# A hybrid attention layer on one core: queries and keys loaded, and chunked outputs stored, 128 partitions at a time

## The reference, cut to what matters

```
proj = x @ w_in                               # aq ak av ag | bq bk bv bg
ya = chunked attention(aq, ak, av, rel_bias)  # 8 heads of 64, own chunk of 64 + 8 before it
ya = ya * silu(ag)
yb = sliding attention(rope(bq), rope(bk), bv, sinks)   # 8 heads, 2 key/value heads, own chunk + 1 before it
yb = yb * silu(bg)
h  = alpha * x + concat(ya, yb) @ w_out
h  = h + sigmoid(h @ w_gate) * (p @ w_ple)
x  = layer_norm(h)
```

## Time and profile before

| | us |
|---|---|
| median of three runs | 2729.72 (2725.06 to 2730.3) |
| the profiled execution | 2724.94 |
| its span, from the first to the last instruction | 2723.1 |
| TensorE busy in the span | 2592.7 (95%) |
| VectorE busy | 1216.6 (45%) |
| ScalarE busy | 1003.4 (37%) |
| GpSimd busy | 354.4 (13%) |
| mean granted TensorE clock | 0.976 |

### The profile page before, as it was taken

The page is one execution under the profiler, slowest core; times in us unless marked ns, Lnnn a source line. Parts: engine busy times, 40 slices in busy tenths (PEclk is TensorE's granted clock), DMA queues, the critical chain, the costliest instruction groups (busy, mean ns, idle before and its releaser), DMA issues. The chain is left out here.

```text
span 2723.1 us, 38119 instructions
## 1 busy us (share of the span) xinstructions
PE 2592.7 (95%) x14100; PEld 2265.4 (83%) x14100; DVE 1216.6 (45%) x2433; ACT 1003.4 (37%) x2091; POOL 354.4 (13%) x192
## 2 busy tenths in 40 slices
PE   7999999999999999998989998887899999999997
PEld 5888888998888888998989897885688888888886
DVE  5211136341212164167878785775334334334333
ACT  4111112241111122167878786774322222222222
POOL 2000000000000000000000000001343443443441
PEclk9999999999999999999999998888999999999998
DMA  6431246363322265388778769987444444445440
GB/s 199 153 123 65 81 97 137 140 229 116 123 89 73 81 116 147 127 217 199 175 167 195 167 149 216 215 224 198 117 123 112 119 118 117 118 114 122 117 112 31
DMA packets 366843, 377.08 MB, mean 138 GB/s; under 512 B 82920, under 2 KB 291960, under 8 KB 363000
## 3 DMA queue, kind: packets, MB, share of 16 engines
q1 hardware_dynamic: 365816, 374.61, 51.9%
q0 software_dynamic: 896, 0.80, 0.1%
HBM read 240.33 MB, written 136.07 MB: 138 GB/s over the span
## 5 line engine op out<-in xcount | busy, mean ns | idle before, releaser
L1347 PE MATMUL psum<-x_hi,w_hi 128*128 128x512 f32 x1344 | 524.1, 390 | 18.1 <-DVE x_lo L1051 17.7
L1347 PE MATMUL psum<-x_lo,w_hi 128*128 128x512 f32 x1344 | 523.8, 390 | 0.0
L1347 PE MATMUL psum<-x_hi,w_lo 128*128 128x512 f32 x1344 | 523.8, 390 | 0.0
L1347 PEld LDWEIGHTS psum<-x_hi,w_hi 128*128 128x128 f32 x1344 | 252.9, 188 | 70.9 <-issue 17.7
L1347 PEld LDWEIGHTS psum<-x_hi,w_lo 128*128 128x128 f32 x1344 | 252.8, 188 | 52.7
L1347 PEld LDWEIGHTS psum<-x_lo,w_hi 128*128 128x128 f32 x1344 | 252.8, 188 | 52.5
L724 POOL TENSOR_TENSOR y_raw<-y_two 128x512 f32<-128x512 f32 x32 | 41.2, 1286 | 1802.8 <-DMA y_two<-ya_d 1802.8
L1148 DVE CUSTOM_DVE_ANT_0 prob<-psum,bias 128x640 f32<-128x640 f32 (+4 forms) x256 | 199.3, 778 | 91.0 <-issue 90.7
L856 ACT ACTIVATE prob<-prob,small 128x640 f32<-128x640 f32 (+4 forms) x256 | 203.9, 797 | 69.4 <-DVE small L1148 65.2
L1245 DVE TENSOR_TENSOR y_lo<-y_raw,y_hi 128x1024 fp32r<-128x1024 f32 x32 | 39.2, 1226 | 397.1 <-ACT y_hi L885 397.1
L1347 PE MATMUL psum<-wo_hi,y_hi 128*128 128x512 f32 x512 | 202.7, 396 | 1.4 <-DVE wo_lo L1240 1.3
(11 more groups left out here) (163 smaller groups left out, 4878.4 us busy)
## 6 DMA issues: line engine op xcount, KB each, us to landing
qk_d<-stage_out SPq DMA_DIRECT2D x72, 512.0 KB, 2.7
w_raw<-in_w_in SPq DMA_DIRECT2D x20, 1024.0 KB, 5.7
v_d<-stage_out SPq DMA_DIRECT2D x64, 320.0 KB, 2.2
x_raw<-in_xT SPq DMA_DIRECT2D x32, 512.0 KB, 4.8
g_d<-stage_out SPq DMA_DIRECT2D x64, 256.0 KB, 2.0
bq_d<-stage_out SPq DMA_DIRECT2D x64, 256.0 KB, 4.0
ya_d<-y_a SPq DMA_DIRECT2D x128, 128.0 KB, 3.6
bq<-bq_d SPq DMA_DIRECT2D x64, 256.0 KB, 5.4
```

The lines of the kernel that those rows point to most:

```text
L1347: return pe.matmul(dst, lhs, rhs, start=start, stop=stop)
```

## The change

Five transfers or pairs of transfers are redrawn. The semaphores count fewer landings accordingly.

- `load_job`: `aq_hi` and `aq_lo` are each loaded by one transfer that reads every row of the source twice, into neighbouring partitions (a copy dimension of 2 behind the 64 rows). `ak` is loaded by one transfer that puts the high and the low part of a row into neighbouring partitions. Partition order is thus (row, copy) in place of (copy, row), alike for both operands. Four transfers per head or part in place of seven. `aq_lo` is now issued at q = 7 together with the bias.
- `load_bq` and `load_bk`: the same for the sliding stage, one transfer in place of two each.
- The store of `y_a`: all 128 partitions in one transfer, to a scratch tensor `ya_d[head, 128, tokens]`.
- `load_tile`: `y_two` is fetched in four transfers of 64 partitions each, in place of one of 128. Its free dimension is ordered (half, pair) in place of (pair, half), and GpSimd's addition reads it so.

```diff
-        ya_d = scratch("ya_d", [A_HEADS // 2, 2, 2, HEAD, SEQ])
+        ya_d = scratch("ya_d", [A_HEADS, 2 * HEAD, SEQ])
...
             def load_job(head, s, piece, done, t0=0, t1=NT):
 
                 cols = slice(t0 * P, t1 * P)
-                if piece < 4:
-                    dst, c, r0 = ((aq_hi, 0, 0), (aq_hi, 0, HEAD), (aq_lo, 1, 0), (aq_lo, 1, HEAD))[piece]
-                    sp.dma_start(dst[r0:r0 + HEAD, s, cols].bitcast(f32), qk_d[c, bass.ds(head * HEAD, HEAD), cols]
+                n = (t1 - t0) * P
+                if piece < 2:
+                    dst = (aq_hi, aq_lo)[piece]
+                    sp.dma_start(dst[:, s, cols].bitcast(f32),
+                                 qk_d[piece, bass.ds(head * HEAD, HEAD), cols].unsqueeze(1).to_broadcast([HEAD, 2, n])
                                  ).then_inc(done, 16)
-                elif piece < 6:
-                    c = piece - 4
-                    sp.dma_start(ak[c * HEAD:c * HEAD + HEAD, s, cols].bitcast(f32),
-                                 qk_d[c, bass.ds(D_A + head * HEAD, HEAD), cols]).then_inc(done, 16)
+                elif piece == 2:
+                    sp.dma_start(ak[:, s, cols].bitcast(f32),
+                                 qk_d[:, bass.ds(D_A + head * HEAD, HEAD), cols].rearrange("c d t -> d c t")
+                                 ).then_inc(done, 16)
...
-                for piece in range(7):
+                for piece in range(4):
...
-                for c in range(2):
-                    sp.dma_start(bq[c * HEAD:c * HEAD + HEAD, which, block * 2 * TB:(block + 1) * 2 * TB].bitcast(f32),
-                                 bq_d[pair + which, :, s * JB + block, c, :, :, :].rearrange("d n h q -> d (n h q)")
-                                 ).then_inc(bq_loaded[block], 16)
+                sp.dma_start(bq[:, which, block * 2 * TB:(block + 1) * 2 * TB].bitcast(f32),
+                             bq_d[pair + which, :, s * JB + block, :, :, :, :].rearrange("d c n h q -> d c (n h q)")
+                             ).then_inc(bq_loaded[block], 16)
...
-                    for r0 in (0, HEAD):
-                        sp.dma_start(dst[r0:r0 + HEAD, s, cols].bitcast(f32), src).then_inc(bk_loaded[s], 16)
+                    sp.dma_start(dst[:, s, cols].bitcast(f32),
+                                 src.unsqueeze(1).to_broadcast([HEAD, 2, cols.stop - cols.start])).then_inc(bk_loaded[s], 16)
...
                         sp.wait_ge(y_copied, quad0 + q + 1)
-                        for c in range(2):
-                            sp.dma_start(ya_d[bass.ds(it, 1), c, s, :, q * TB:q * TB + TB]
-                                         .rearrange("a d t -> (a d) t"),
-                                         y_a[c * HEAD:c * HEAD + HEAD, q % QSLOTS, :]).then_inc(y_stored[q % QSLOTS], 16)
+                        sp.dma_start(ya_d[bass.ds(head, 1), :, q * TB:q * TB + TB].rearrange("a d t -> (a d) t"),
+                                     y_a[:, q % QSLOTS, :]).then_inc(y_stored[q % QSLOTS], 16)
...
-                sp.dma_start(y_two[:, s, :, :], ya_d[:, :, :, :, cols].rearrange("k c h d t -> (h d) (k c) t")
-                             ).then_inc(y_two_loaded[s], 16)
+                for hd in range(2):
+                    for c in range(2):
+                        sp.dma_start(y_two[hd * HEAD:hd * HEAD + HEAD, s, c * KT // 2:(c + 1) * KT // 2, :],
+                                     ya_d[:, c * HEAD:c * HEAD + HEAD, cols].rearrange("(k h) d t -> h d k t", h=2)[hd]
+                                     ).then_inc(y_two_loaded[s], 16)
```

More of the change, by code:

```diff
@@ L283, in wait_head @@
                 if t % PART == 0:
-                    eng.wait_ge(first_loaded[t // PART], 16 * (9 if t == 0 else 7))
+                    eng.wait_ge(first_loaded[t // PART], 16 * (6 if t == 0 else 4))
             elif t == 0:
-                eng.wait_ge(job_loaded[s], 144 * (turn + s))
+                eng.wait_ge(job_loaded[s], 96 * (turn + s))
         def v_out(slot):
@@ L299, in _ @@
             for sm in y_stored:
-                sp.sem_inc(sm, 32)
+                sp.sem_inc(sm, 16)
             def load_panel(col, width):
@@ L500, in stage_a @@
                         sp.wait_ge(y_copied, quad0 + q + 1)
-                        for c in range(2):
-                            sp.dma_start(ya_d[bass.ds(it, 1), c, s, :, q * TB:q * TB + TB]
-                                         .rearrange("a d t -> (a d) t"),
-                                         y_a[c * HEAD:c * HEAD + HEAD, q % QSLOTS, :]).then_inc(y_stored[q % QSLOTS], 16)
+                        sp.dma_start(ya_d[bass.ds(head, 1), :, q * TB:q * TB + TB].rearrange("a d t -> (a d) t"),
+                                     y_a[:, q % QSLOTS, :]).then_inc(y_stored[q % QSLOTS], 16)
                         if q == 0 and more:
-                            load_job(head + 1, 1 - s, 4, job_loaded[1 - s])
-                            load_job(head + 1, 1 - s, 5, job_loaded[1 - s])
+                            load_job(head + 1, 1 - s, 2, job_loaded[1 - s])
                         if q == 1 and more:
-                            load_job(head + 1, 1 - s, 6, job_loaded[1 - s])
+                            load_job(head + 1, 1 - s, 3, job_loaded[1 - s])
                         if q == QUADS - 2 and load_next:
@@ L515, in stage_a @@
                             load_job(head + 2, s, 0, job_loaded[s])
+                        if q == QUADS - 1 and load_next:
                             load_job(head + 2, s, 1, job_loaded[s])
-                        if q == QUADS - 1 and load_next:
-                            load_job(head + 2, s, 2, job_loaded[s])
-                            load_job(head + 2, s, 3, job_loaded[s])
                             load_bias(head + 2, s, job_loaded[s])
@@ L540, in _ @@
                 first_head(part)
-            for piece in range(4):
+            for piece in range(2):
                 load_job(1, 1, piece, job_loaded[1])
@@ L547, in _ @@
             for stored in y_stored:
-                sp.wait_ge(stored, 32 * (A_HEADS * QUADS // QSLOTS + 1))
+                sp.wait_ge(stored, 16 * (A_HEADS * QUADS // QSLOTS + 1))
             sp.wait_ge(recipT_copied, 1)
@@ L718, in y_tile @@
             def y_tile(t, s, first=False):
-                two = y_two[:, s, :, :].rearrange("p (k c) t -> p k c t", c=2)
-                pool.wait_ge(y_two_loaded[s], 8 * (t - s) + 16)
+                two = y_two[:, s, :, :].rearrange("p (c k) t -> p c k t", c=2)
+                pool.wait_ge(y_two_loaded[s], 32 * (t - s) + 64)
                 if not first:
                     pool.wait_ge(y_split, t - 1)
-                pool.tensor_tensor(y_raw[:, s, 0:KT // 2, :], two[:, :, 0, :], two[:, :, 1, :], ALU.add).then_inc(y_joined, 1)
+                pool.tensor_tensor(y_raw[:, s, 0:KT // 2, :], two[:, 0, :, :], two[:, 1, :, :], ALU.add).then_inc(y_joined, 1)
                 pool.wait_ge(g_loaded[s], 8 * (t - s) + 16)
@@ L845, in a_step @@
                     act.wait_ge(values_done, A_QUADS * it + quad + 1)
-                    act.wait_ge(y_stored[slot], 32 * (A_QUADS // QSLOTS * it + quad // QSLOTS + 1))
+                    act.wait_ge(y_stored[slot], 16 * (A_QUADS // QSLOTS * it + quad // QSLOTS + 1))
                     act.activation(y_a[:, slot, :], psum[:, 6 + quad % 2, :], ACT.Copy).then_inc(y_copied, 1)
@@ L1472, in b_scores @@
                 if u % 4 == 0:
-                    pe.wait_ge(bq_loaded[i // 2], 64 * (u // (2 * B_UNITS) + 1))
+                    pe.wait_ge(bq_loaded[i // 2], 32 * (u // (2 * B_UNITS) + 1))
                 if i == 0:
-                    pe.wait_ge(bk_loaded[s], 64 * (pair // 2 + 1))
+                    pe.wait_ge(bk_loaded[s], 32 * (pair // 2 + 1))
                 if u >= 2:
```

## The result

| | before | after |
|---|---|---|
| median, us | 2727.39 (2724.75 to 2730.3, 4 runs) | 2701.3 (2696.57 to 2701.87, 4 runs) |
| the profiled execution, us | 2724.94 | 2701.23 |
| its span, us | 2723.1 | 2699.4 |
| TensorE busy, us | 2592.7 | 2586.1 (96%) |
| mean granted clock | 0.976 | 0.979 |

The ratio is 0.990, 95% interval 0.9883 to 0.9918: some 26 us by the medians, 23.7 by the two profiled executions. The forecast was 2700, in a range of 2690 to 2719.

What follows compares the result with a forecast made beforehand. Slow 64-partition transfers were held to make TensorE wait in the chunked and sliding stages. Terms -11.1 -1.5 -20 +2.5 = -30 us: 2695 from the profiled 2724.94, 2700 from the median 2729.72; range 2690 to 2719.

Steps and rivals of the forecast that it cites:

- The mechanism: Query and key loads, y_a stores: a busy engine moves 1.6 to 1.9 times as much when transfers span 128 partitions.
- First head and first change: Chunked stage, first head and change to the second: the wait for av and both y_a waits go; gain 11.1 us.
- Start of the sliding stage: TensorE's 4.2 us wait for bq shrinks as its load is issued sooner and moves quicker; gain 1.5 us.
- Body of the sliding stage: VectorE's waits for y_b stores mostly go, and the slower clock with them; gain 20 us, bounds 10 and 22.5.
- at 1745 about 1 us stays: Sliding body: the 4.1 us wait for a y_b store behind bq and v_b shrinks to about 1 us.
- the wait at 1791: Sliding body: a 2.5 us wait for a y_b store was to go (4 us less bq).
- under 3 us: Sign to look for: VectorE's y_b waits before 1840 us total under 3 us.
- y_two in four: End of sliding stage and changeover: three more issues per tile lose 1.25 us at each, together 2.5; steady tiles cost 0.
- 1 (issues only): All changed transfers: width buys no rate, only issues are saved; about 2721 us, chance 0.10.
- 3 (the twice-read source): Loads of aq_hi and aq_lo: copying one HBM place to many partitions is slow; near 2900 us, chance 0.05.
- 2 (the small-run loads are the true cause): SyncE's queue: v_b's and av's 4096 pieces fill it and stay; body gains only 4 to 6; 2715 us, chance 0.11.
- 4 (the last stage): Last stage: the y_two fetch comes onto its path, 31 tiles by 1 us; about 2730 us, chance 0.04.

Runs made afterwards that it cites:

- the kernel with the old count: Against the kernel before: query and key loads 128 partitions wide but cut in two by columns, as many transfers as before, outputs as before; 2701.75 us.
- the kernel with v_b in two: Against the changed kernel: each group's middle v_b load in two parts by columns, the second three steps later; 2697.1 us.

## Why the prediction was right

- *The mechanism.* Forecast: width pays in rate, by the y_a and stage_out rows. Shown, by the kernel with the old count (2701.75) and by that with every second partition (415 GB/s). The wording "two engines sharing a way into one half" is more than was shown; shown is that loads into one half move 218 GB/s at a full share, and loads over both 415 to 422.
- *First head and first change, -11.1.* Measured -11.05, and av's wait is gone; av landed at 1211.98, forecast was 1213. Fewer issues were not needed for it: with the old count the four passes take 28.00 as well.
- *Start of the sliding stage, -1.5.* Measured -2.6; bq's wait went from 4.2 to 2.5, where 2.7 was named. With the loads alone wide it was 3.2, so the single store of y_a has its share in it, as forecast.
- *Body of the sliding stage, -20 within 10 to 22.5.* Measured -14.2. This is the mis-sized term. The step that failed is the last: "at 1745 about 1 us stays", and that the wait at 1791 goes. Both v_b waits stayed, at 1.88 and 2.34 us; their 4.2 us also miss the sign "under 3 us". I had subtracted bq's saving from the old wait. But v_b's issue waits for TensorE's progress, so it doesn't move ahead. What to add up was the queue ahead of the store: 1 MB of bq (3 us at 341 GB/s) and 2 MB of v_b in 512-byte runs (7 us at the 299 of the earlier trace rows). That is 10 us, before the store's own 2 to 3, where the slot is wanted again after two passes, 9.4. With the rate of the strips in the earlier trace rows for bq, this was to be had from the rows. The clock was not the error: 1 us of wait was priced at 2.5 us lost, and 4.2 us of wait left 8.4. Mis-sized was what waits. As the body with slow loads took 121.65 to 125.63 us and with wide ones 106.34 to 108.96, the gain is some 13 to 19 us and the -14.2 of one pair of executions is near its lower end.
- *y_two in four, +2.5.* Two places were to lose 1.25 each. Measured +2.3 at the end of the sliding stage, where the kernels with four transfers lie 2.4 above those with one, and nothing that shows at the changeover: its gap went from 11.98 to 12.15 and the first tile grew by 0.7, but with one transfer and wide loads they are as long or longer (13.38, and 27.05 for the tile's 26.54). The sum is right by luck, as one place was twice as dear and the other free. The gap was named at 12.5 to 14 and stayed under it. In the steady tiles y_two took 3.0 to 3.4 us to issue where it took 0.39, more than the 1.2 to 2.0 added in the forecast, and r_c left some 1.3 us later behind it, not 0.5; the tiles did not grow, as forecast.
- *The sum.* -30 against the profiled execution's 2724.94. Measured -23.7, of which the body's error is 5.8 and the loop passes, which I had left alone, 3.3; what I had put down to the outputs took 0.7 more than forecast; start, head and end give 3.4 back. The total of 2701.3 looks closer to 2700 than the terms were, and part of that is luck in the base: 2700 was 30 us under a median of 2729.72, and the kernel before has 2727.39 in the result. From there the forecast is 2697, and the gain by the medians is 26 of 30.
- *Rivals.* 1 (issues only) and 3 (the twice-read source) are shown wrong. 2 (the small-run loads are the true cause) holds for 8.4 of the 22.5 us of the body, as the kernel with v_b in two shows, and not for the first change. 4 (the last stage) did not come.

## What to carry to other kernels

When the DMA share is high, divide GB/s by it for each kind of transfer; if one kind moves half as much per busy engine, look where in the partitions it lands before you look at its bytes. Let each transfer span both halves of the partitions, with the 64 rows in front and the copy behind; the order of these two dimensions decides between a gain of 1% and a loss of 24%. For a store behind a load in an in-order queue, add up the bytes ahead of it since the last event that the queue waited for, and compare that with the time until its slot is wanted.

## What the runs showed of the hardware that I had not expected

- Two engines alone moved 53 GB/s, 26.5 each; sixteen moved 422, 26.4 each. An engine of a wide load is as fast in company as with one neighbour (a 16 KB packet took 613 ns both times), while in transfers to one half of the partitions it made 13.6 (218 over 16).
- A transfer of 64 rows to every second partition is as fast as one of 128 (415 GB/s, packets of 16 KB in 612 ns).
- 4.2 us of waits in two pieces cost 8.4 us, as the granted clock fell to 0.63 to 0.69 in the 8 us behind each, and stayed at 1.00 where they were gone.
